# A two-block transformer on one core: modulation rows on one ring and partly on VectorE, and another order in the second attention

## The reference, cut to what matters

```python
# first block: one hybrid layer, then rmsnorm
z = rmsnorm(h) @ w_in                    # q, k, v, u (SSM input), two gates
attn = dilated_band_attention(...)       # three groups of four heads
y = gelu(s5_ssm(u, ...))                 # state-space layer
h = h + (gate_a * (attn @ w_attn_proj) + gate_s * (y @ w_glu_a) * sigmoid(y @ w_glu_b)) @ w_out
h = h + (silu(n2 @ w_ffn_gate) * (n2 @ w_ffn_up)) @ w_ffn_down
h = h + sigmoid(h @ w_ple_gate) * (p @ w_ple_proj)
# second block: two layers on x = rmsnorm(h) and a context of the same size
for i in range(2):
    mod_l = split(silu(c) @ w_mod[i] + b_mod[i], 6)       # six rows of 1024 for x
    mod_c = split(silu(c_ctx) @ w_mod[i] + b_mod[i], 6)   # six for the context
    hl = rms_norm(xl) * (1 + mod_l[1]) + mod_l[0]
    ol = conv_module(hl) if i == 0 else gqa_mixer(hl, hc) # 31-tap depthwise conv / 16 heads over 4 kv heads
    xl = xl + mod_l[2] * ol
    hl = rms_norm(xl) * (1 + mod_l[4]) + mod_l[3]
    xl = xl + mod_l[5] * (relu(hl @ w_ff1[i]) ** 2 @ w_ff2[i])
    # the same for the context in layer 0; in layer 1 it only gives keys and values
```

## Time and profile before

| what | us |
|---|---|
| three runs | 1541.20, 1542.08, 1542.18 |
| median | 1542.08 |
| profiled execution, its own time | 1542.83 |
| its span, first to last instruction | 1541.0 |
| mean granted TensorE clock in it | 0.978 |
| TensorE busy | 1457.1 |
| VectorE busy | 757.9 |
| ScalarE busy | 593.9 |
| GpSimd busy | 405.7 |

### The profile page before, as it was taken

How to read it: one execution, slowest core, us unless ns; L and a number is a source line. 1 busy time by engine, 2 the same in 40 slices (tenths; PEclk the granted TensorE clock), 3 DMA queues, 4 the chain that set the end, 5 groups by cost and what they waited for, 6 DMA issues and landing times.

```text
span 1541.0 us, 25205 instructions
## 1 busy us (share of the span) xinstructions
PE 1457.1 (95%) x10880; PEld 1253.1 (81%) x10880; DVE 757.9 (49%) x977; ACT 593.9 (39%) x725; POOL 405.7 (26%) x324
## 2 busy tenths in 40 slices
PE   5799999988999997999799999999999989899999
PEld 5688889988999996765276888888887855899999
DVE  7975645365545467566556121212124577453343
ACT  4433364434333455121245222322223447544443
POOL 4977712100002410000000333343230020134553
PEclk9899999999999998999899999999999989999999
DMA  7466676554655564876434323232223310346452
GB/s 257 164 219 211 220 242 219 203 161 137 191 176 180 191 219 170 266 229 188 127 132 159 115 82 109 82 110 85 106 96 124 97 66 4 110 137 191 172 184 82
DMA packets 158259, 239.37 MB, mean 155 GB/s; under 512 B 5680, under 2 KB 128592, under 8 KB 158032
## 3 DMA queue, kind: packets, MB, share of 16 engines
q1 hardware_dynamic: 153360, 232.85, 45.6%
q10 hardware_dynamic: 4800, 5.08, 1.3%
HBM read 227.55 MB, written 1.05 MB: 148 GB/s over the span
## 4 chain that ended last, share of the span: by engine, by line
PE 86%; DVE 7%; ACT 4%; issue 2%; DMA 1%; POOL 0%; DVEq 0%; SPq 0%; ACTq 0%; POOLq 0%
PE bank L1976 25%; PE bank L1977 24%; PE bank L1978 24%; PE bank L2281 2%; PE bank L2044 2%; DVE wlo L1083 1%; ACT whi L631 1%; PE bank L2441 1%; PE bank L2118 1%; DVE stat L1721 1%; PE bank L562 1%; PE bank L543 1%; PE bank L2153 1%; PE bank L2083 1%; PE bank L2288 0%
## 5 line engine op out<-in xcount | busy, mean ns | idle before, releaser
L1976 PE MATMUL bank<-ahi,whi 128*128 128x256 f32 (+1 forms) x2480 | 792.3, 319 | 38.5 <-DVE wlo L1083 10.1
L1977 PE MATMUL bank<-alo,whi 128*128 128x256 f32 (+1 forms) x2480 | 783.8, 316 | 0.0
L1978 PE MATMUL bank<-ahi,wlo 128*128 128x256 f32 (+1 forms) x2480 | 783.8, 316 | 0.0
L1083 DVE TENSOR_TENSOR wlo<-raw,whi 128x2048 fp32r<-128x2048 f32 x158 | 362.2, 2292 | 534.5 <-ACT whi L631 534.3
L631 ACT ACTIVATE whi<-raw 128x2048 fp32r<-128x2048 f32 x160 | 306.3, 1914 | 727.6 <-PE bank L1978 727.6
L1976 PEld LDWEIGHTS bank<-ahi,whi 128*128 128x128 f32 x2480 | 478.0, 193 | 83.9 <-issue 40.7
L1978 PEld LDWEIGHTS bank<-ahi,wlo 128*128 128x128 f32 x2480 | 477.8, 193 | 28.6
L1977 PEld LDWEIGHTS bank<-alo,whi 128*128 128x128 f32 x2480 | 478.5, 193 | 27.7 <-issue 0.2
L1914 POOL TENSOR_TENSOR alo<-A,ahi 128x512 fp32r<-128x512 f32 (+1 forms) x43 | 125.8, 2928 | 351.8 <-ACT ahi L831 351.8
L1932 POOL TENSOR_TENSOR A<-A 128x512 f32 (+1 forms) x48 | 96.6, 2026 | 442.1 <-ACT A L954 442.1
L1568 DVE SCALAR_TENSOR_TENSOR A<-A,decay 128x512 f32<-128x512 f32 x80 | 53.7, 742 | 0.0
(11 more groups left out here) (301 smaller groups left out, 1200.0 us busy)
## 6 DMA issues: line engine op xcount, KB each, us to landing
raw<-in_w_ff SPq DMA_DIRECT2D x64, 1024.0 KB, 5.2
A<-in_w_mod SPq DMA_DIRECT2D x60, 512.0 KB, 4.6
raw<-in_w_in SPq DMA_DIRECT2D x28, 1024.0 KB, 8.0
modraw<-in_w_mod SPq DMA_DIRECT2D x36, 512.0 KB, 4.6
raw<-in_pw SPq DMA_DIRECT2D x12, 1024.0 KB, 7.2
raw<-in_w_ffn_gate SPq DMA_DIRECT2D x11, 1024.0 KB, 5.3
raw<-in_w_ffn_up SPq DMA_DIRECT2D x11, 1024.0 KB, 5.3
raw<-in_w_ffn_down SPq DMA_DIRECT2D x11, 1024.0 KB, 4.9
```

Of the source, the lines that this page charges most:

```text
L1083: dve.tensor_tensor(wlo[:, k % 2, :], raw[:, (k + 2) % 4, :], whi[:, k % 2, :].bitcast(F32), ALU.subtract).then_inc(wlo_ready, 1)
L1976: pe.matmul(out_, w_hi, a_hi, start=start, stop=False, **kw)
L1977: pe.matmul(out_, w_hi, a_lo, start=False, stop=False, **kw)
L1978: return pe.matmul(out_, w_lo, a_hi, start=False, stop=stop, **kw)
```

## The change

It has three parts.

**Modulation.** The ring `modraw` goes, and all 96 pieces, g = 0 to 95, go through the ring of four, in the order of rows `MOD_ROW`. None is used during "in" any more. Six of the 12 rows (n = 0, 1, 6, 7, 8, 9) are summed on VectorE: `mod_on_dve(g)` does two operations per piece, one for each of x and context, over 128 x 1024 (a `tensor_scalar` for the first piece of a row, then `scalar_tensor_tensor`), into an area `MOD_SUM[n]` of SBUF. Such a row is then summed over the partitions on TensorE by `mod_collect(n)`, eight fp32 matmuls of 256 columns with a matrix `pickrow`, and goes on through `mod_rows`, `mod_turn` and `store_mods` as before. VectorE's pieces: 0 to 10 in "ffn", one per pair of blocks; 11 to 15 in blocks 0 to 4 of "down"; 48 to 71 in "ff1a", two per block in blocks 0 to 11; 72 to 79 in "ff2a", one per block in blocks 0 to 7. Collections: behind blocks 1 and 7 of "down", 5, 9 and 13 of "ff1a", and behind "ff2a". The other six rows stay on TensorE: pieces 16 to 19 at the end of ple, 20 to 31 behind blocks 1 to 6 of pw1, 32 to 35 among the channel sums, 36 to 47 around pw2, 80 to 87 around the norm behind "ff2a", 88 to 95 around the norm behind "wo". SyncE's loads follow; ff1a, VectorE's ffn and ff2a are written out instead of rolled into loops; the masks get an area of their own and are loaded at block 6.

**"in".** `output_powers(0)` moves from ahead of VectorE's loop to behind the splits at l = 2 and 3, and `output_powers(1)` to l = 4 and 5. `ssm_y(c)` moves one block back, to l = 9, 12, 15 and 18.

**Second attention.** `pg` has three buffers, and exp of step i waits for the transposition of step i-3 and not i-2. For even i from 4 on, VectorE (`gptb`) copies the second half of the transposed probabilities. GpSimd's two splits go: VectorE does them at i = 17 and behind the loop. ScalarE's whi for the second block of "wo" moves to i = 10.

```diff
-MOD_ORDER = [0, 1, 2, 4, 5, 3]
-MOD_BANK = [6, 6, 6, 6, 4, 2]
-TURN_BANK = [7, 7, 7, 7, 5, 7]
+MOD_ROW = [(0, 0), (0, 1), (0, 2), (0, 3), (0, 4), (0, 5), (1, 0), (1, 1), (1, 2), (1, 4), (1, 3), (1, 5)]
+MOD_BANK = [2, 2, 6, 6, 6, 4, 0, 0, 0, 3, 2, 5]
+TURN_BANK = [3, 3, 7, 7, 7, 5, 1, 1, 1, 7, 7, 6]
+MOD_SUM = {0: 14336, 1: 18432, 6: 12288, 7: 14336, 8: 18432, 9: 18432}
+MOD_COLLECT = [0, 1, 6, 7, 8, 9]
...
-        pg = area(9728, 2048).rearrange("p (r a w) -> p r a w", r=2, a=2)
+        pg = area(13824, 3072).rearrange("p (r a w) -> p r a w", r=3, a=2)
...
SyncE
+            def load_mod(g):
+
+                if g >= 4:
+                    sync.wait_ge(modraw_used, g - 3)
+                n, c = divmod(g, KD)
+                layer, m = MOD_ROW[n]
+                sync.dma_start(modraw1[g % 4], I["w_mod"][layer][P * c:P * c + P, D * m:D * m + D])\
+                    .then_inc(modraw1_landed[g % 4], 16)
...
-                        if 4 <= l:
-                            load_mod(0, 2 * (l - 4))
-                            load_mod(0, 2 * (l - 4) + 1)
...
+                if name == "ffn":
+                    for l in range(22):
+                        load(name, Pos(FIRST[name] + l, l))
+                        if l == 0 or l % 2:
+                            load_mod((l + 1) // 2)
+                    continue
...
                 if name == "pw1":
-                    for t in range(4):
-                        load_mod(1, t)
+                    for g in range(16, 20):
+                        load_mod(g)
                     for l in range(4):
                         load(name, Pos(FIRST[name] + l, l))
-                    for t in range(4, 8):
-                        load_mod(1, t)
+                    for g in range(20, 24):
+                        load_mod(g)
...
                     for l in range(8):
-                        load_mod(1, 12 + 2 * l)
-                        load_mod(1, 13 + 2 * l)
+                        if 1 <= l <= 5:
+                            load_mod(22 + 2 * l)
+                            load_mod(23 + 2 * l)
...
ScalarE
-                    if i >= 2 and b == 0:
-                        act.wait_ge(pt_done, TR + i - 1)
+                    if i >= 3 and b == 0:
+                        act.wait_ge(pt_done, TR + i - 2)
...
-                for s in range(2):
-                    c = act.activation(ptg[:, i % 2, 512 * s:512 * s + 512], pb[4 + s][:, :], ACT.Copy)
-                c.then_inc(pt_ready, 1)
+                for s in range(1 if copied_on_dve(i) else 2):
+                    act.activation(ptg[:, i % 2, 512 * s:512 * s + 512], pb[4 + s][:, :], ACT.Copy).then_inc(pt_ready, 1)
...
VectorE
-            dve.wait_ge(z_ready, 1)
-            dve.wait_ge(ssm_landed, 32)
-            output_powers(0, 3, 8)
...
-                if l in (3, 4):
-                    output_powers(1, *((3, 5), (5, 8))[l - 3])
+                if l == 2:
+                    dve.wait_ge(z_ready, 1)
+                    dve.wait_ge(ssm_landed, 32)
+                if 2 <= l < 6:
+                    output_powers((l - 2) // 2, *((3, 5), (5, 8))[l % 2])
...
+            def mod_on_dve(g):
+
+                n, c = divmod(g, KD)
+                dve.wait_ge(modraw1_landed[g % 4], 16 * (g // 4 + 1))
+                dve.wait_ge(modraw_used, g)
+                if n == 9 and c == 0:
+                    dve.wait_ge(mod_summed, 5)
+                for s in range(2):
+                    a = area(MOD_SUM[n] + D * s, D)
+                    w = scc[:, 2 * c + s:2 * c + s + 1]
+                    if c == 0:
+                        i = dve.tensor_scalar(a, modraw1[g % 4], w, None, ALU.mult)
+                    else:
+                        i = dve.scalar_tensor_tensor(a, modraw1[g % 4], w, a, ALU.mult, ALU.add)
+                i.then_inc(modraw_used, 1)
...
+            def gptb(i):
+                dve.wait_ge(pt_done, TR + i + 1)
+                dve.wait_ge(o_done, TR + i - 1)
+                dve.tensor_copy(ptg[:, i % 2, 512:1024], pb[5][:, :]).then_inc(pt_ready, 1)
...
+                if i - 3 < GSTEPS and copied_on_dve(i - 3):
+                    gptb(i - 3)
                 if 0 <= i - 2 < GSTEPS:
                     gscale(i - 2)
...
+                if i == GSTEPS + 1:
+                    ahead(Pos(FIRST["qkv"] + 4, 4))
+            ahead(Pos(FIRST["qkv"] + 5, 5))
             ph[0] = "wo"
-            dve.wait_ge(wlo_ready, FIRST["wo"] + 2)
...
GpSimd
-            split_ahead(4)
-            split_ahead(5)
...
TensorE
+            def mod_collect(n):
+
+                pe.wait_ge(modraw_used, KD * (n + 1))
+                for s in range(2):
+                    for q in range(4):
+                        x0 = MOD_SUM[n] + D * s + 256 * q
+                        mm = pe.matmul(pb[MOD_BANK[n]][32 * q:32 * q + 32, 0:256], pickrow[:, 1 - s:33 - s],
+                                       area(x0, 256), start=(s == 0), stop=(s == 1))
+                mm.then_inc(mod_summed, 1)
...
-                if 2 <= l < 26:
-                    if l == 2:
-                        pe.wait_ge(silu_ready, 1)
-                    if l % 4 == 2 and l > 2:
-                        mod_turn(0, (l - 6) // 4)
-                    mod_piece(0, 2 * (l - 2))
-                    mod_piece(0, 2 * (l - 2) + 1)
...
-                if l in (8, 11, 14, 17):
-                    ssm_y((l - 8) // 3)
+                if l in (9, 12, 15, 18):
+                    ssm_y((l - 9) // 3)
...
-                if l == 0:
-                    mod_pieces(4, 4)
-                mod_pieces(8 + 2 * l, 2)
+                if l == 4:
+                    mod_turn(2)
+                if 1 <= l < 7:
+                    mod_pieces(18 + 2 * l, 2)
             convolve(4)
             pe.wait_ge(u_ready, KD)
             for c in range(2):
                 channel_sum(c)
             convolve(5)
-            for c in range(2, 4):
+            for c in range(2, 5):
                 channel_sum(c)
+            mod_turn(3)
+            mod_pieces(32, 2)
+            channel_sum(5)
             convolve(6)
-            mod_turn(1, 2)
-            mod_pieces(24, 2)
             convolve(7)
-            channel_sum(4)
-            channel_sum(5)
-            mod_pieces(26, 2)
             channel_sum(6)
+            mod_pieces(34, 2)
             channel_sum(7).then_inc(msum_done, 1)
```

More of the change, by code:

```diff
@@ L220, in program @@
         chunks_free = sem("chunks_free")
-        modraw_landed = [sem(f"modraw_landed{n}") for n in range(2)]
+        mod_summed = sem("mod_row_summed")
         modraw1_landed = [sem(f"modraw1_landed{n}") for n in range(4)]
@@ L476, in _ @@
                             shift_copies(sync, l // 2, 2)
-                    for t in range(28, 36):
-                        load_mod(1, t)
+                    for g in range(34, 44):
+                        load_mod(g)
                     sync.wait_ge(conv_done, KD)
@@ L484, in _ @@
                 if name == "ff1a":
-                    for l in range(8):
+                    for l in range(16):
                         load(name, Pos(FIRST[name] + l, l))
                         if l == 3:
-                            for t in range(36, 44):
-                                load_mod(1, t)
-                    each_block(sync, name, lambda p: load(name, p), first=8)
+                            for g in range(44, 48):
+                                load_mod(g)
+                        if l >= 4:
+                            load_mod(40 + 2 * l)
+                            load_mod(41 + 2 * l)
+                    continue
+                if name == "ff2a":
+                    for l in range(16):
+                        load(name, Pos(FIRST[name] + l, l))
+                        if 2 <= l < 14:
+                            load_mod(70 + l)
                     continue
@@ L495, in _ @@
                         if l == 3:
-                            for t in range(44, 48):
-                                load_mod(1, t)
+                            for g in range(84, 88):
+                                load_mod(g)
+                    continue
+                if name == "wo":
+                    for g in range(88, 92):
+                        load_mod(g)
+                if name == "ff1b":
+                    for l in range(8):
+                        load(name, Pos(FIRST[name] + l, l))
+                        if l == 3:
+                            for g in range(92, 96):
+                                load_mod(g)
+                    each_block(sync, name, lambda p: load(name, p), first=8)
                     continue
@@ L970, in body @@
                             hidden_hi(l, 0, 16, w, hid, u_at, l)
+                    if name == "ff1a" and p.least in (6, 10, 14):
+                        mod_rows(6 + (p.least - 6) // 4)
                     relus(p)
+                    if name == "ff1b" and p.least == 0:
+                        mod_rows(11)
                 ph[0] = name
```

(37 more changed lines are left out.)

190 lines of the change are left out of this document (102 added, 88 removed).

## The result

The changed kernel takes 1526.67 us (median of four runs, 1523.39 to 1528.37) against 1541.78 for the kernel before on the same chips: ratio 0.9899, interval 0.9884 to 0.9914. It is 15 us faster. The direction was right, and 1505.3 with its range of 1494 to 1519 was wrong: less than half of the 36.8 us came. The profiled execution is the slowest of the four (1528.37); its span is 1526.6, 14.4 less than before.

What follows compares the result with a forecast made beforehand. TensorE, busy 95% of the span and 86% of the chain, was taken as the bound. Terms -21.0 + 2.9 - 11.4 - 6.0 + 4.3 + 1.0 + 0.4 - 7.0 gave -36.8: 1505.3 us, range 1494 to 1519.

Steps and rivals of the forecast that it cites:

- The pieces out of "in" (-20.4): In "in", 19 groups of modulation pieces on TensorE's chain go, -19.0 us, and four turns, -1.4.
- the start (-3.0): Start of "in": TensorE's 9.82 us wait shrinks as output_powers(0) moves behind wlo of block 4; surplus -3.0, bounds 0 and -12.2.
- bounds 0 (GpSimd's power chain holds it back): Start of "in": the bound at which GpSimd's power chain leaves nothing of the start's -3.0 us surplus.
- The first three only move: In "in": the first three ssm_y, placed one block later, merely move, at no cost.
- The last y: In "in": the last ssm_y, now behind block 18, delays attention's first maximum and exp, and whi(20): +2.4 us, bounds 0 and +4.
- pw1 (-11.4): In pw1: pieces and a DMA wait between blocks 0 and 1, the low clock and one turn go; bounds -6 and -12.5.
- Convolution (-6.0): Tail of the convolution: convolve(6) waits 1.2 and runs 4.29, 11.5 us instead of 17.9 in all; bounds -3 and -7.
- Sums on VectorE (0): In ffn, ff1a, ff2a and down: 48 pieces, about 2.5 us each, are hidden beside VectorE's other work; cost 0.
- collects (+2.9, +4.3): Collecting summed rows on TensorE, 1.00 us each plus turns of 0.44: two in down +2.9, three in ff1a +4.3.
- Second attention (-7.0): GpSimd's split and low clock go, -5.5; steady steps -2.5; against it +0.6 and +0.4; bounds -4 and -10 us.
- wo and ff1b (0): Pieces lie in TensorE's waits; +0.3 for late sums, +0.4 for a turn, up to -2 if the clock stays up; taken 0.
- the second rival: Waits return: half of the 24.4 us of pw1, convolution and attention reappears, 1517.5 us, range 1512 to 1528; chance 0.18.

Runs made afterwards that it cites:

- powers_first: Changed kernel with output_powers(0) back ahead of VectorE's loop and output_powers(1) at l = 3 and 4; median 1526.15 us, ratio to before 0.9899.
- short_pool: Changed kernel with two of three steps of GpSimd's powers of chunk 1 left out; one run, 1524.44 us.
- all_five: Changed kernel with the edits of row11, powers_first, y17, rows2_first and ScalarE's split for wo at step 18; median 1511.93 us, ratio to before 0.9812.
- all_five_y8: all_five with all four ssm_y back behind blocks 8, 11, 14 and 17, as before the change; 1525.77 us, ratio to before 0.9882.
- y17: Changed kernel with only the last ssm_y back behind block 17 of "in"; median 1524.21 us, ratio to before 0.9893.
- rows2_first: Changed kernel with ScalarE's copy of row 2 ahead of its split at block 3 of pw1; median 1523.03 us, ratio to before 0.9877.
- no_pieces: Changed kernel with VectorE's sums, except each row's first piece, run over 16 of 1024 columns; 1527.99 us.
- row11: Changed kernel with pieces 88 to 91 behind block 1 of wo and row 11's turn one block later; median 1522.15 us, ratio to before 0.9879.
- filler: Changed kernel with eight further idle fp32 matmuls on TensorE behind each of blocks 18, 19 and 20 of "in"; median 1526.57 us, ratio to before 0.9894.

## Why the prediction was wrong, point by point

**The pieces out of "in" (-20.4) and the start (-3.0).** The step that failed is "bounds 0 (GpSimd's power chain holds it back)": I named GpSimd as a bound and took it to cost at most the start's surplus. It costs more than that surplus, since every later block that TensorE gains brings it nearer to GpSimd. Before, GpSimd's powers of chunk 1 were ready at 95.8 and wanted at 109.2. In the changed kernel they are wanted at 96.5 and ready at 101.7, since two more splits fell inside GpSimd's chain. `powers_first`, with one more than before, tells the two apart: one came in because TensorE runs earlier and so calls VectorE's splits earlier, the other because the powers no longer stood ahead of the first of them. `short_pool` shows that chain as the bound, the table of held operations what stretches it. "Block 8 starts at 89.3" was nearly right (the turn behind it, which comes about 6.8 after that start, was wanted at 96.5); what had to be ready for it was not looked at. The term for the pieces held: with VectorE's powers and the last y in their old places `all_five` has "in" at -20.4 against before, and -20.4 was what the 19 groups and the turns were to give. (Five of the six turns stood on the chain and not four, 0.3 more.) The term for the start had the wrong sign. -3.0 was taken, and `powers_first` gives back about 3 by undoing the move. The waits also came elsewhere than forecast: not 5 and 4 us for wlo of blocks 6 and 8, but 4.3 for VectorE's rotation (L1327), 3.4 and 5.3 for GpSimd, and 0.8 for wlo.
The Trainium skill ("SBUF — State Buffer", section "Who interferes with whom") has the port pair of VectorE and GpSimd as an exclusive lock. I weighed it for the sums on VectorE, where I made 1 us of it, and not for GpSimd's chain. The trace agrees with it in the direction that I left out: beside a split, which has two inputs in SBUF, 0.46 grew to 3.10. The row at 1261.16, on which the prediction leaned, has only one such tensor. And it was GpSimd's operation that waited though it had begun before the split (51.02 against 51.53).

**ssm_y.** "The first three only move" priced the move rightly and missed what it was for: left behind blocks 8, 11 and 14, y would have stood for GpSimd (`all_five_y8`). The last y was sized +2.4 in all, 1.4 of it lateness of whi(20); `y17` gave back 2.7, about 2.0 of it that lateness and the rest the wait and the clock behind it. The mechanism was right.

**pw1 (-11.4).** The wait for the load, the half clock and the pieces went: -10.5 up to block 1, 0.9 short of the forecast. What failed is that nothing was put for the bank that rows 2 and 3 share: piece 24 waits for the copy of row 2, which stood behind a split, 2.3 (`rows2_first`).

**Convolution (-6.0).** -6.3, from the steps that were forecast: the chain has 1.43 of waiting (forecast 1.2) and then two chunks in 8.79, 4.4 each.

```profile
719.56 1.43 issue
720.99 8.79 PE bank L2362 x80
```

**Sums on VectorE (0), collects (+2.9, +4.3).** Hidden, as forecast (`no_pieces`), although a sum took 1.79 us on the mean of 60. A collect with its turn cost 1.7 to 1.8 in ff1a instead of 1.44.

**Second attention (-7.0).** -5.0. Of the 2.0 that are short, 0.9 is a term that was mis-sized: the 0.4 put for ScalarE's split at step 10 was 1.3. Another 1.3 is the low clock at the first steps, which four other traces of the same code do not have. The scaling (L1730 before, L1804 now) lost its long wait, as forecast: 15.1 us for 32 instead of 19.4.

**wo and ff1b (0).** The largest single miss, 8.8, and the second step that failed. The step "up to -2 if the clock stays up. I take 0" treats the pieces' loads as landed. The ring has four buffers: pieces 92 to 95 can be loaded only when 88 to 91 have been used, at 1320. The four loads are issued from 1320.8 on and take 4.9 us (median of three) and 8.4; TensorE stands behind them and slows. I had costed the matmuls, not when their loads could start, and not that row 11's turn would wait for ScalarE. `row11` shows it: 6.4 came back, and the 2.3 that remain against before are mostly the 1.9 of pieces 88 to 91.

**"glu" to "ffn" (+1.5).** This is scatter and no effect of the change. `filler` and `all_five_y8` have the same code there and take 195.8 us, 2.0 less than the changed kernel's trace and 0.5 less than before. The waits are about the same in all. The granted clock was 0.89 from 310.9 to 320.9 in the changed kernel, and 1.00 at the same place in the other two and before.

**The rivals.** 1526.67 lies in the range of the second rival (1512 to 1528), but not for its reason. Pw1, convolution and attention, which it had bring half of 24.4, brought 19.4. What was lost lay in "in" and behind wo, which no rival had as a loss.

## What to carry to other kernels

Work taken off the bounding engine is worth only the distance to the next one: measure for each dependence when it is ready and when it is wanted, for helpers that hold 0% of the chain too. A load's price is when its buffer comes free, so write down for each ring the use that releases the slot. A small copy that something waits for belongs ahead of the long operation on its engine, not behind it: that order alone was worth 2.4 us in pw1, and part of the 6.4 behind wo.

## What the runs showed of the hardware

GpSimd's operations of 128x128 took 0.46 us where VectorE was idle and 3.1 to 3.4 where VectorE's 128x2048 subtraction (2.27) began half a microsecond behind them, and it lost nothing by that. Where the subtraction had begun first, the operation took 2.2 to 2.7 and the subtraction up to 2.65. The size hardly counted: one of 128x16 took 3.29, one of 128x512 3.69. VectorE's sums lost too: two of them took 2.5 us with GpSimd idle and 3.5 to 4.6 beside its 128x512 operations.

The granted clock fell behind waits of 5 to 6 us in "in": to 0.52 for 100 to 105, and to 0.50 and 0.56 for 214 to 217 and 217 to 220. With 3 us of further matmuls behind blocks 18 to 20 (`filler`) it fell all the same, to 0.57 and 0.50 for the same stretches. In `y17`, behind a wait of 5.0, it was 0.58 for 214 to 217 and back at 1.00 for 217 to 220.
